# The rope's exchange of halves: a product with a signed permutation, or four transfers per head and kind

## The chip, the cores and the metric

The kernel runs on one core of a Trainium2 chip. The time is that of the device in microseconds (us); less is better. A core has TensorE (PE) for matrix products, VectorE (DVE), ScalarE (ACT) and GpSimd (POOL) for work on elements, and SyncE (SP), which here only sends transfers. ACT sends transfers too, from a queue of its own. Sums of products stand in PSUM, eight banks of 128 x 512 f32; everything else in SBUF, 128 partitions wide.

## The reference

Two layers of a transformer block with three branches over a latent sequence of 512 tokens and a context of 256: a gated convolution of 31 taps, a bidirectional chunked delta rule, and differential attention with 4 heads of two 64-wide parts. The change is in attention, in the rotary embedding (rope) of q and k, which only the 512 latent tokens get:

```python
def apply_rope(x, cos, sin):
    xf = x.astype(jnp.float32)
    half = xf.shape[-1] // 2
    rot = jnp.concatenate([-xf[..., half:], xf[..., :half]], axis=-1)
    return (xf * cos[:, None, None, :] + rot * sin[:, None, None, :]).astype(x.dtype)

    (conv_val, conv_glu, conv_z, dq, dk, dv, dz, dbeta, ddecay,
     aq, ak, av, az, mgate) = jnp.split(h @ w_in, IN_SPLITS, axis=-1)
    ...
    q_lat = apply_rope(qk_heads(aq, da_q_norm_g), cos, sin)
    k_lat = apply_rope(qk_heads(ak, da_k_norm_g), cos, sin)
    v_lat = av.reshape(B, S, DA_HEADS, 2 * DA_HEAD)
    o_da = diff_attention_latent(q_lat, k_lat, v_lat, k_ctx, v_ctx, lam)
    ...
    x_new = x + gate[:, None] * merge_branches(ys, mgate, w_branch, w_out)
```

`qk_heads` is an RMS norm over the 64 elements of each part. Within such a part rope needs the 32 elements of the one half beside those of the other, the sign of one of them turned.

## The kernel before

Channels lie on the partitions, tokens along the free axis. So one head's q is a tile of 128 partitions (two parts of 64) by 768 columns (512 latent tokens and 256 of context; in layer 1 the context has no q), and the exchange of halves moves rows of 32 partitions: 0-31 with 32-63, 64-95 with 96-127.

**Weights.** The projections are "units": one unit is 128 output channels, for which 512 KB of weights come by one transfer from SP into one of four buffers (`raw`, L845). ACT rounds them to a high part (`wHs`, L872), POOL or DVE takes the rest as a low part (`wLs`, L1973 on POOL in two halves, L1506 on DVE), and `dense` (L506) makes three products for each of eight blocks of input channels, 24 matmuls of 512 columns and, where the context belongs to it, as many of 256. A unit can start when both parts are there and the bank that it takes has been read. SP sends the weights of a unit when PE has ended the one four units before.

**Banks.** `product` (L417 to L435) gives every product the next one or two of the eight PSUM banks in turn and waits on PE until the bank's last product has been read by whoever reads it. The product of the exchange takes one bank in this round.

**One head.** For head h of layer l there are units for q, k and v; sums of squares per part (`allsum`, L521, with a block matrix) and their root on ACT (table loads L861, Ln L879, Exp L886); the norm on DVE (`an`, L1901) in place in `qh` or `kh`, which have two buffers each, by h % 2; and then the step `qrot`, the rope:
- PE: one product of the signed permutation `rot` with q or k (L798; the profile counts a 128x512 f32 product here as two instructions).
- DVE: `gm` = that product times the sine (L1911), reading the bank; it waits until the last use of `gm` is over.
- POOL: q or k times the cosine in place (L2095), then plus `gm` (L2098).

Cosine and sine are the table `cs`, loaded once per layer (L1210). Scores of a head (L552) wait for the rope of its q and k. Around them stand the softmax (maxima L1464 and L1467 on DVE, exponentials L906 on ACT, the mix L1488 and L1491 on DVE), the turn of the mixed weights (L529, copied by ACT at L1386 to `aT`), the product with the values (L565, copied by DVE at L484).

**Order.** `schedule` (L104 to L178) writes one list of steps for the whole program, and every engine walks the same list and issues its part of each step, so an engine's queue is in this order. While head h attends, the units and steps of head h + 1 are put in between: "q", "k", "sq", "v", "rq" (the exchange of q), "sk", "t", "rk" (the exchange of k). In these slots stand gate units too, whose logits are either made sigmoids of (L1240) or parked: ACT copies them (L1264) and sends them to DRAM (L1266), 256 or 384 KB. In layer 0 heads 2 and 3 get their exchanges beside parked units and pieces of the modulation vectors (`ada`, L999, L1444), in layer 1 "rq", "sk" and a parked unit are one slot, and "t", a parked unit and "rk" the next. ACT runs ahead of its steps where it prepares weights (`ahead`), as POOL does.

## Time and profile before

| | |
|---|---|
| runs (3), median | 1927.29 us |
| lowest, highest | 1923.66, 1928.23 us |
| profiled execution | 1927.93 us |
| its span | 1926.1 us |
| its mean granted TensorE clock | 0.973 of full speed |
| busy PE, DVE, ACT, POOL | 1799.3, 1127.7, 971.5, 669.2 us |
| bytes moved by transfers | 178.86 MB, 93 GB/s over the span |

Read it so. PE is busy nearly all the time, so both what PE does and what makes it wait set the end. The heads of attention are made in two stretches, about 485 to 835 us and 1495 to 1745 us from the span's start. Times of rows are starts from the start of the span; "[2.72 <-ACT Pa L906]" behind a row means that the engine stood idle so long before it, and what released it. A row without such brackets followed its forerunner on that engine at once.

### The profile page before, as it was taken

The page shows a single profiled execution, that of the slowest core. Times are in us where ns is not written, and L with a number is a line of the kernel's source. Part 1 is how long each engine was busy: PE and PEld are TensorE (multiplying, and loading weights), DVE is VectorE, ACT ScalarE, POOL GpSimd, SP SyncE. Part 2 cuts the span into 40 slices and gives each one's busy share as a digit, 9 for nine tenths or more (in the row PEclk, how much of TensorE's full clock was granted, in tenths as well). Part 3 has the DMA queues.
Part 4 walks back from the last instruction along what each step waited for, and adds up shares of the span by engine and source line. Part 5 has one row for each costly group of instructions (what it writes and reads, how often), then busy time and mean ns, then how long its engine had stood idle before and what let it go on. Part 6 is the DMA issues. An engine that isn't in the chain of part 4 may idle for free. (4 is left out here: it accounts for less than half of the span.)

```text
span 1926.1 us, 27717 instructions
## 1 busy us (share of the span) xinstructions
PE 1799.3 (93%) x11060; PEld 1497.2 (78%) x11060; DVE 1127.7 (59%) x1610; ACT 971.5 (50%) x1297; POOL 669.2 (35%) x490
## 2 busy tenths in 40 slices
PE   6789996899999999999999978999798999999999
PEld 5678886898888888888788857878696787777777
DVE  5556495459667656553234255749759866465343
ACT  6657523336445455553653156753337564555661
POOL 0011421537743434453153000144346544433150
PEclk9899998999999999999999999999799999999999
DMA  7123224422221122233244213324222221212352
GB/s 300 34 77 110 72 72 146 133 67 59 95 77 44 55 72 75 82 104 116 89 129 163 96 54 96 98 78 121 78 67 66 77 66 55 72 50 91 106 186 87
DMA packets 76414, 178.86 MB, mean 93 GB/s; under 512 B 6464, under 2 KB 29312, under 8 KB 76160
## 3 DMA queue, kind: packets, MB, share of 16 engines
q1 hardware_dynamic: 34272, 122.46, 20.6%
q10 hardware_dynamic: 42016, 54.63, 8.3%
q8 instruction: 89, 1.46, 0.3%
q14 instruction: 37, 0.30, 0.0%
HBM read 156.00 MB, written 21.07 MB: 92 GB/s over the span
## 5 line engine op out<-in xcount | busy, mean ns | idle before, releaser
L506 PE MATMUL banks<-hH,wHs 128*128 128x512 f32 x1984 | 599.0, 364 | 46.9 <-DVE hL L474 20.5
L506 PE MATMUL banks<-hH,wLs 128*128 128x512 f32 x1984 | 582.8, 355 | 0.0
L506 PE MATMUL banks<-hL,wHs 128*128 128x512 f32 x1984 | 581.1, 355 | 0.0
L1973 POOL TENSOR_TENSOR wLs<-raw,wHs 128x512 fp32r<-128x512 f32 x272 | 410.8, 1536 | 465.2 <-ACT wHs L872 465.2
L506 PEld LDWEIGHTS banks<-hH,wHs 128*128 128x128 f32 x1984 | 327.0, 191 | 123.6 <-issue 26.1
L506 PEld LDWEIGHTS banks<-hL,wHs 128*128 128x128 f32 x1984 | 324.8, 191 | 55.5 <-issue 2.2
L506 PEld LDWEIGHTS banks<-hH,wLs 128*128 128x128 f32 x1984 | 324.6, 191 | 54.7
L872 ACT ACTIVATE wHs<-raw 128x1024 fp32r<-128x1024 f32 x210 | 219.7, 1053 | 219.4 <-DMA raw<-wstream 219.2
L1529 DVE SCALAR_TENSOR_TENSOR acc<-padc,vecs,acc 128x783 f32<-128x783 f32 (+1 forms) x240 | 294.6, 1281 | 0.0
L861 ACT ACT_TABLE_LOAD x180 | 230.9, 1283 | 30.2 <-issue 13.0
L906 ACT ACTIVATE Pa<-banks,stat 128x768 f32<-128x768 f32 (+1 forms) x80 | 64.6, 813 | 144.0 <-DVE stat L1467 144.0
L1506 DVE TENSOR_TENSOR wLs<-raw,wHs 128x1024 fp32r<-128x1024 f32 x74 | 90.9, 1232 | 14.6 <-ACT wHs L872 14.5
L506 PE MATMUL banks<-yH,wHs 128*128 128x512 f32 (+1 forms) x288 | 89.8, 366 | 4.2 <-DVE gm L1850 1.8
L506 PE MATMUL banks<-yH,wLs 128*128 128x512 f32 (+1 forms) x288 | 88.0, 360 | 0.0
L506 PE MATMUL banks<-yL,wHs 128*128 128x512 f32 (+1 forms) x288 | 88.0, 360 | 0.0
L1464 DVE TENSOR_REDUCE stat<-banks 128x1 f32<-128x768 f32 (+1 forms) x80 | 64.0, 840 | 15.3 <-PE banks L552 15.1
L2079 POOL TENSOR_TENSOR mT<-mT,gm 128x768 f32<-128x768 f32 (+1 forms) x32 | 58.7, 1842 | 36.9 <-DVE gm L1850 36.9
L1193 ACT ACTIVATE vn<-banks,bcol 128x128 f32<-128x128 f32 x96 | 26.1, 381 | 77.8 <-DVE vs L1780 77.8
L1949 DVE SCALAR_TENSOR_TENSOR xs<-banks,ada,xs 128x512 f32<-128x512 f32 (+1 forms) x24 | 15.1, 658 | 83.2 <-PE banks L506 83.2
L552 PE MATMUL banks<-kh,qh 64*128 64x256 f32 (+1 forms) x288 | 55.6, 499 | 5.8 <-issue 5.6
L506 PEld LDWEIGHTS banks<-yH,wHs 128*128 128x128 f32 x288 | 47.9, 189 | 15.6 <-issue 3.9
L1491 DVE SCALAR_TENSOR_TENSOR Pa<-Pa,stat,Pa 128x768 f32<-128x768 f32 (+1 forms) x40 | 59.0, 1476 | 1.4
(242 smaller groups left out, 2330.8 us busy)
## 6 DMA issues: line engine op xcount, KB each, us to landing
raw<-wstream SPq DMA_DIRECT2D x210, 512.0 KB, 3.6
araw<-wstream SPq DMA_DIRECT2D x16, 512.0 KB, 12.6
E<-g_rows ACTq DMA_DIRECT2D x16, 384.0 KB, 7.0
egb<-eg_rows ACTq DMA_DIRECT2D x20, 256.0 KB, 4.2
inb<-intra_rows ACTq DMA_DIRECT2D x20, 256.0 KB, 4.5
parked_logits<-sg ACTq DMA_DIRECT2D x13, 384.0 KB, 4.1
xs<-xT SPq DMA_DIRECT2D x8, 384.0 KB, 11.4
intra_rows<-E ACTq DMA_DIRECT2D x8, 384.0 KB, 3.1
```

Of the source, the lines that this page charges most:

```text
L506: last = pe.matmul(out[:, a:b], w, m[:, kt, a:b], start=(kt == 0 and j == 0), stop=(kt == kts - 1 and j == 2))
L552: last = pe.matmul(outs[m][:, o:o + b - a], q_[r, qt * P:(qt + 1) * P], k_[r, a:b], start=True, stop=True)
L861: act.add_instruction(mybir.InstLoadActFuncSet(name=nc.get_next_instruction_name(), act_func_set_id=FUNCTION_SET[f], ins=[], outs=[]))
L872: act.activation(wH[w % RING][:, :], raw[w % RING][:, :], ACT.Copy).then_inc(*tick("act", "hi", v))
L906: act.activation(Pa[i][m][:, 0:w], place[key][:, 0:w], ACT.Exp, bias=stat[:, i, 2 + m:3 + m], accum_out=stat[:, i, 4 + m:5 + m]).then_inc( ...
L1193: ins = act.activation(vn[d][:, h, :], place[key][:, h * P:(h + 1) * P], ACT.Copy, scale=bcol[:, ORDER[d][s], 4 * d + h:4 * d + h + 1])
L1464: dve.tensor_reduce(stat[:, i, m:m + 1], place[key][:, 0:w], AX_X, ALU.max).then_inc(*tick("dve", "mx", l, h, qt, m))
L1491: dve.scalar_tensor_tensor(Pa[i][0][:, 0:w], Pa[i][0][:, 0:w], stat[:, i, 6:7], Pa[i][1][:, 0:w], ALU.mult, ALU.add).then_inc(*tick("dve", ...
L1506: dve.tensor_tensor(wL[w % RING][:, :], raw[w % RING][:, :], wH[w % RING][:, :].bitcast(F32), ALU.subtract).then_inc(*tick("dve", "lo", v))
L1529: ins = dve.scalar_tensor_tensor(acc[:, t, 0:W], padc[:, t, k:k + W], w, acc[:, t, 0:W], ALU.mult, ALU.add)
L1973: ins = pool.tensor_tensor(wL[w % RING][:, o:o + 512], raw[w % RING][:, o:o + 512], wH[w % RING][:, o:o + 512].bitcast(F32), ALU.subtract)
L2079: pool.tensor_tensor(mT[:, d, 0:n], mT[:, d, 0:n], gms[d % 2][:, 0:n], ALU.add).then_inc(*tick("pool", "gadd", l, n_, d))
```

## The change

The permutation and its product are gone. At the same step ACT now sends four transfers, each of 32 partitions by 512 tokens (64 KB), from `qh` or `kh` straight into `gm`, the half of one part into the place of the other: `o ^ 32` is the other half's first partition. Before them it waits for the norm of this tile (`an`), for the end of the rope before this one (the last reader of `gm`), and at the first exchange of layer 1 for an older use of the buffer. DVE waits for the fourth transfer and multiplies `gm` by the sine in place, POOL waits for that. The sign is in the sine table now, made on the host beside the other constants. PE has nothing to do at this step and takes no bank.

```diff
@@ -48,7 +48,7 @@
 NV = V_AL + 1

-C_ID, C_BLK, C_ROT, C_NEG = 0, 128, 256, 384
+C_ID, C_BLK, C_NEG = 0, 128, 256
 NCON = C_NEG + 2 * P
@@ -237,7 +237,7 @@
         stages = ["start"] + sorted({it[0] for it in ITEMS})
         names = ["%s_%s" % (e, k) for e in ("pe", "act", "dve", "pool") for k in stages]
-        names += ["w_high", "w_low_pool", "w_low_dve", "raw0", "raw1", "raw2", "raw3", "small_in", "c_in", "x_in", "x_out", "rope_in"]
+        names += ["w_high", "w_low_pool", "w_low_dve", "raw0", "raw1", "raw2", "raw3", "small_in", "c_in", "x_in", "x_out", "rope_in", "halves_in"]
         names += ["park_out0", "park_out1", "leaf_out0", "leaf_out1"] + ["park_in%d" % i for i in range(4)]
@@ -307,7 +307,6 @@
         ident = cons[:, C_ID:C_ID + P]
         blk = cons[:, C_BLK:C_BLK + P]
-        rot = cons[:, C_ROT:C_ROT + P]

@@ -791,12 +790,7 @@
                            lambda t: ("asq", kind, l, h), 1)
                 elif k == "qrot":
-                    h, kind = it[2], it[3]
-                    dst = (qh if kind == "aq" else kh)[h % 2]
-                    out = product(pe, ("rot", kind, l, h), SEQ)
-                    pe.wait_ge(*done("an", kind, l, h))
-                    pe.matmul(out[:, 0:SEQ], rot, dst[:, 0:SEQ], start=True,
-                              stop=True).then_inc(*tick("pe", "pe", ("rot", kind, l, h)))
+                    pass
                 elif k == "vunit":
@@ -850,6 +844,7 @@
             done_hi = [0]
             prev_ada = []
+            last_rope = []
             first_hi = [0]
@@ -1351,6 +1346,18 @@
                         act.wait_ge(*done("read", ("ak", l, h), 0))
                         act.activation(at1[0][:, 0:n], kh[h % 2][:, 0:n], ACT.Square).then_inc(*tick("act", "asq", "ak", l, h))
+                elif k == "qrot":
+                    h, kind = it[2], it[3]
+                    src = (qh if kind == "aq" else kh)[h % 2]
+                    act.wait_ge(*done("an", kind, l, h))
+                    if last_rope:
+                        act.wait_ge(*done("rope", *last_rope[-1]))
+                    if l and not (h or kind == "ak"):
+                        act.wait_ge(*done("gadd", l - 1, 0, KT - 2))
+                    last_rope.append((kind, l, h))
+                    for o in range(0, P, 32):
+                        act.dma_start(gm[o:o + 32, 0:SEQ], src[o ^ 32:(o ^ 32) + 32, 0:SEQ]).then_inc(
+                            *tick("halves_in", "half", kind, l, h, o, by=16))
                 elif k == "vunit":
@@ -1902,14 +1909,11 @@
                 elif k == "qrot":
                     h, kind = it[2], it[3]
-                    key = ("rot", kind, l, h)
-                    dve.wait_ge(*done("pe", key))
+                    dve.wait_ge(*done("half", kind, l, h, 96))
                     dve.wait_ge(*done("rope_in", l))
-                    if last_gm[0]:
-                        dve.wait_ge(*done(*last_gm[0]))
                     last_gm[0] = ("rope", kind, l, h)
-                    dve.tensor_tensor(gm[:, 0:SEQ], place[key][:, 0:SEQ], cs[:, 1, :],
-                                      ALU.mult).then_inc(*tick_read("dve", key))
+                    dve.tensor_tensor(gm[:, 0:SEQ], gm[:, 0:SEQ], cs[:, 1, :],
+                                      ALU.mult).then_inc(*tick("dve", "rots", kind, l, h))
                 elif k == "sc":
@@ -2091,7 +2095,7 @@
                     h, kind = it[2], it[3]
                     dst = (qh if kind == "aq" else kh)[h % 2]
-                    pool.wait_ge(*done("read", ("rot", kind, l, h), 0))
+                    pool.wait_ge(*done("rots", kind, l, h))
                     pool.tensor_tensor(dst[:, 0:SEQ], dst[:, 0:SEQ], cs[:, 0, :],
@@ -2169,12 +2173,6 @@
     con[:, C_ID:C_ID + P] = np.eye(P)
     con[:, C_BLK:C_BLK + P] = (i[:, None] // 64) == (i[None, :] // 64)
-    for m in range(P):
-        if m % 64 < 32:
-            con[m + 32, C_ROT + m] = -1.0
-        else:
-            con[m - 32, C_ROT + m] = 1.0
-
     con[:, C_NEG:C_NEG + P] = np.where(i[:, None] <= i[None, :], 0.0, -1e30)
@@ -2184,7 +2182,8 @@
     ang = np.concatenate([ang, ang], axis=-1).T
     ang = np.concatenate([ang, ang], axis=0)
-    rope = np.stack([np.cos(ang), np.sin(ang)], axis=1).astype(np.float32)
+    sign = np.where(i[:, None] % 64 < 32, -1.0, 1.0)
+    rope = np.stack([np.cos(ang), sign * np.sin(ang)], axis=1).astype(np.float32)
     return {"con": con, "rope": rope}
```

ScalarE's order in layer 1 where head 2's q is exchanged (`qh_164` is that q, `Pa` the softmax weights, `at` the root, `wHs` a unit's high part, `sg` parked logits), before:

```order
L906 ACTIVATE Pa_176,stat<-banks,stat 128x768 [waits pe_pv,dve_sc]
L906 ACTIVATE Pa_177,stat<-banks,stat 128x768 [waits pe_pv,dve_sc]
L861 ACT_TABLE_LOAD [waits dve_qsum]
L879 ACTIVATE at_1_172<-banks,misc 128x768 [waits pe_qsum]
L861 ACT_TABLE_LOAD
L886 ACTIVATE at_1_172<-at_1_172 128x768 [waits act_qsum]
L872 ACTIVATE wHs<-raw_52 128x1024 [waits pe_vunit,raw1]
L1264 ACTIVATE sg_137<-banks 128x512 [waits dve_branch,pe_park]
L1266 DMA parked_logits<-sg_137 128x512 [waits act_park]
```

and with the change:

```order
L901 ACTIVATE Pa_176,stat<-banks,stat 128x768 [waits pe_pv,dve_sc]
L901 ACTIVATE Pa_177,stat<-banks,stat 128x768 [waits pe_pv,dve_sc]
L1359 DMA gm<-qh_164 32x512 [waits pool_qrot,dve_qsum]
L1359 DMA gm<-qh_164 32x512 x3
L856 ACT_TABLE_LOAD [waits dve_qsum]
L874 ACTIVATE at_1_172<-banks,misc 128x768 [waits pe_qsum]
L856 ACT_TABLE_LOAD
L881 ACTIVATE at_1_172<-at_1_172 128x768 [waits act_qsum]
L867 ACTIVATE wHs<-raw_52 128x1024 [waits pe_vunit,raw1]
L1259 ACTIVATE sg_137<-banks 128x512 [waits dve_branch,pe_park]
L1261 DMA parked_logits<-sg_137 128x512 [waits act_park]
```

The four issues stand behind the exponentials and ahead of the table load for k's root; all that follows keeps its order.

TensorE's order at the same place (`L552` are the scores of head 1, `L521` the sum of squares of k, `L506` the unit behind them), before:

```order
L552 MATMUL banks<-kh_167,qh_165 128x512 [waits pool_qrot,act_vunit,act_qunit,act_qsum]
L552 MATMUL banks<-kh_167,qh_165 128x512
L552 MATMUL banks<-kh_167,qh_165 128x256 x2
L798 MATMUL banks<-qh_164,cons 128x512 [waits dve_qsum,act_pv]
L521 MATMUL banks<-at_0_171,cons 128x512 [waits act_qsum,act_sc,dve_pv]
L521 MATMUL banks<-at_0_171,cons 128x256
L506 MATMUL banks<-hH,wHs 128x512 [waits w_low_pool,w_high,act_sc]
```

and with the change, where these lines are L551, L520 and L505:

```order
L551 MATMUL banks<-kh_167,qh_165 128x512 [waits pool_qrot,act_vunit,act_qunit,act_qsum]
L551 MATMUL banks<-kh_167,qh_165 128x512
L551 MATMUL banks<-kh_167,qh_165 128x256 x2
L520 MATMUL banks<-at_0_171,cons 128x512 [waits act_qsum,act_pv]
L520 MATMUL banks<-at_0_171,cons 128x256
L505 MATMUL banks<-hH,wHs 128x512 [waits w_low_pool,w_high,dve_pv]
```

The product is gone, and with the round of banks moved by one the sum of squares and the unit wait for other readers: `dve_pv` is DVE's copy at L484, `act_sc` the exponentials, `act_pv` the copy of `aT`.

## Rows read from the trace of the kernel before

**Rows 1.** Page, section 1: busy us (share of the span) and instructions per engine.
```profile
PE 1799.3 (93%) x11060; PEld 1497.2 (78%) x11060; DVE 1127.7 (59%) x1610; ACT 971.5 (50%) x1297; POOL 669.2 (35%) x490
```

**Rows 2.** Busy us of each engine, summed over eight stretches with exchanges.
```profile
sum 600.00, PE 586.70 PEld 474.12 DVE 374.30 ACT 314.30 POOL 276.58; mean PE 73.34 PEld 59.27 DVE 46.79 ACT 39.29 POOL 34.57
```

**Rows 3.** Chain of waits, 1655 to 1670: start us, us, what.
```profile
1662.10 0.86 PE banks L798 x2
```

**Rows 4.** Timeline of PE, 1641 to 1650: start, us, instruction, idle before.
```profile
1648.22 0.50 PE L506 MATMUL banks<-hH,wHs 128*128 128x512 f32 x1 [2.72 <-ACT Pa L906]
```

**Rows 5.** Transfers: timeline of ACT's issues, query of L1266, page section 6.
```profile
1386.67 0.45 ACTq L955 DMA_DIRECT2D egb<-eg_rows  x1
1387.15 0.47 ACTq L957 DMA_DIRECT2D inb<-intra_rows  x1
...
L1266 ACTq DMA_DIRECT2D parked_logits<-sg x23: 326/326/352, 699.6 to 1786.4; - x23
...
DMA to landing us min/median/max: 2.0/4.1/5.7
...
parked_logits<-sg ACTq DMA_DIRECT2D x10, 256.0 KB, 3.9
```

**Rows 6.** Timelines of four engines, 532 to 545: layer 0, head 0.
```profile
532.87 0.37 ACT L999 ACTIVATE adar<-banks 4x256 f32<-4x256 f32 x1 [1.34 <-PE banks L582]
...
533.87 0.69 DVE L1911 TENSOR_TENSOR gm<-banks,cs 128x512 f32<-128x512 f32 x1 [0.70 <-PE banks L798]
...
538.61 6.50 POOL L1973 TENSOR_TENSOR wLs<-raw,wHs 128x512 fp32r<-128x512 f32 x4
...
543.71 0.61 PE L506 MATMUL banks<-hH,wHs 128*128 128x512 f32 x2
```

**Rows 7.** Timelines of ACT and PE, 609 to 621.5: layer 0, head 1's q.
```profile
618.13 0.81 ACT L1386 ACTIVATE aT<-banks 128x768 f32<-128x768 f32 x1
...
620.39 0.60 PE L506 MATMUL banks<-hH,wHs 128*128 128x512 f32 x2
```

**Rows 8.** Timelines of four engines, 693 to 706: layer 0, head 2's q.
```profile
695.55 1.05 ACT L872 ACTIVATE wHs<-raw 128x1024 fp32r<-128x1024 f32 x1
...
693.69 0.69 DVE L1911 TENSOR_TENSOR gm<-banks,cs 128x512 f32<-128x512 f32 x1
...
697.09 2.54 POOL L1973 TENSOR_TENSOR wLs<-raw,wHs 128x512 fp32r<-128x512 f32 x2
...
704.73 0.71 PE L506 MATMUL banks<-hH,wHs 128*128 128x512 f32 x2
```

**Rows 9.** Timelines of four engines, 1520 to 1529: layer 1, head 0's k.
```profile
1521.11 0.60 ACT L1240 ACTIVATE sg<-banks 128x512 f32<-128x512 f32 x1 [1.52 <-PE banks L506]
...
1521.96 0.69 DVE L1911 TENSOR_TENSOR gm<-banks,cs 128x512 f32<-128x512 f32 x1 [2.58 <-PE banks L798]
...
1524.54 1.64 POOL L2098 TENSOR_TENSOR kh<-kh,gm 128x512 f32<-128x512 f32 x1
...
1527.45 1.56 PE L552 MATMUL banks<-kh,qh 64*128 64x512 f32 x8
```

**Rows 10.** Timelines of ACT and PE, 1646.5 to 1658: layer 1, head 2's q.
```profile
1654.28 0.58 ACT L1264 ACTIVATE sg<-banks 128x512 f32<-128x512 f32 x1
...
1656.37 0.48 PE L506 MATMUL banks<-hH,wHs 128*128 128x512 f32 x1
```

**Rows 11.** Timelines of ACT and PE, 1722 to 1738: layer 1, head 3.
```profile
1723.03 1.04 ACT L872 ACTIVATE wHs<-raw 128x1024 fp32r<-128x1024 f32 x1
...
1734.11 0.33 ACTq L1266 DMA_DIRECT2D parked_logits<-sg  x1
...
1727.71 0.48 PE L506 MATMUL banks<-hH,wHs 128*128 128x512 f32 x1
...
1734.80 2.84 PE L565 MATMUL banks<-aT,Va 128*128 128x128 f32 x24
```

**Rows 12.** Stretch 1718.5 to 1721.9, after a wait: busy, PEclk, DMA share.
```profile
1718.50:1721.90 3.40, 3.40 (x10) 2.66 (x9) 0.00 (x0) 3.35 (x5) 1.61 (x2) 0.50 0.00 0
```

## The prediction

> **What bounds the kernel now.** I read the page first, for the share of each engine. The reader is to see that TensorE (PE) is busy 1799.3 us, 93% of the span, and that no other engine passes 59% [rows 1]. Then I cut out the eight stretches in which the heads of attention are prepared, with the table of busy time by stretch: 600 us in all, in which PE is busy 586.70 us, and VectorE (DVE), ScalarE (ACT) and GpSimd (POOL) 374.30, 314.30 and 276.58 us [rows 2]. So the first question is what goes from PE's row of work, and the second what makes PE wait after it. The timelines of the four engines at each exchange of halves answer the second. The profiled execution took 1927.93 us, 1.83 us more than its span; the sum is made against that, and the median of the runs (1927.29) is 0.64 us below it, less than the runs differ among themselves.
>
> **What goes.** Each exchange takes one product (two matmul instructions) from PE. The chain of waits gives its price where PE stands full before and after it: 0.86 us between two runs of 24 dense matmuls [rows 3]. There are 16 exchanges (two layers, four heads, q and k), so PE gets back 13.8 us at most. The product also took a PSUM bank in turn. Without it the following products meet other predecessors in the round of eight banks; in layer 1 the order shows that the unit behind head 2's exchange waits for an operation of `pv` in place of one of `sc`. Before, PE stands 2.72 us for that exponential [rows 4], and once more the same at head 3. That wait can go as well. What gets late next decides the sum.
>
> **What comes.** ACT issues four transfers of 64 KB, then DVE multiplies by the sine in place, then POOL does its two operations as before. Two sizes matter, and neither operation stands in the trace.
> I is ACT's time for four issues. Issues that follow one another start 0.48 us apart [rows 5], so I = 1.9 us; the single issue at L1266 takes 0.33 us [rows 5], so the lower bound is 4 x 0.33 = 1.3.
> L is the time from the first issue to the landing of the last quarter. Ends: three issues of 0.33 and the fastest landing of a parked block, 2.0 [rows 5], give 3.0; three pitches of 0.48 and its slowest, 5.7, give 7.1. The nearest row is the parked block of the same 256 KB from this queue, 3.9 [rows 5]; so L = 3.9, which leaves 2.5 us for the landing of the last quarter.
> The DVE multiply keeps its length, 0.69 us; its source is now SBUF. Weight loads are in flight at the same moments, since SP sends one whenever PE ends a unit; that is inside the bound of 7.1.
>
> At one place the Trainium skill is to be weighed. The row gives 3.9 for 256 KB in one transfer [rows 5]. "DMA: Bandwidth & Descriptors", section "Anatomy of one DMA — SWDGE (gpsimd) path", puts a transfer at some 2.0 us and its bytes at 436 GB/s, 2.15 us for 64 KB. If the four overlap, an estimate by it is L = 3 x 0.48 + 2.15 = 3.6, and the sum below would be 1.2 us smaller. "SBUF — State Buffer", section "The DMA setup-cost knee", speaks against the change: small transfers pay that fixed part each. Were the four to run one behind the other, L would be 8.6 and the sum 19 us larger. The issues 0.48 us apart show that a queue takes the next without waiting for the landing of the one before.
>
> **The places, one by one** (plus is later).
> Layer 0, head 0, both kinds in one stretch. The last ACT work before k's exchange waits for PE and ends at 533.24; PE comes 0.86 earlier without q's product, so ACT is free at 532.38. The sine multiply starts at 532.38 + 3.9 = 536.28 instead of 533.87, 2.41 later. POOL goes on gapless behind it: rope, then the low parts of weights, of which the unit at 543.71 needs the first two (half of the 6.50 in the row), done at 541.86 before and 544.27 now. Against 543.71: +0.56 [rows 6].
> Layer 0, head 1. At q ACT is gapless up to the copy of aT, done at 618.94; with I it is 620.84, and the unit's bank is that one's, started at 620.39 before: +0.45 [rows 7]. At k nothing is near: -0.86.
> Layer 0, head 2. At q ACT comes to the exchange at 695.55. The multiply moves from 693.69 to 699.45, 5.76 later. POOL's rope and two low parts end at 705.39 instead of 699.63, and PE wanted them at 704.73: +0.66 [rows 8]. What PE had gained before that is given back. k: -0.86. Head 3 of layer 0 has the same pattern, so again +0.66 - 0.86.
> Layer 1, head 0, both kinds. ACT is free at 1521.71 - 0.86 = 1520.85; the multiply starts at 1524.75 instead of 1521.96, 2.79 later; POOL's rope, done at 1526.18, is at 1528.97, and the scores stood at 1527.45: +1.52 [rows 9].
> Layer 1, head 1: both have cover, -1.72.
> Layer 1, head 2. At q ACT is gapless up to the copy of the parked logits, done at 1654.86; with I 1656.76, and the unit whose bank it frees started at 1656.37: +0.39. So the 2.72 us of [rows 4] are not gained, they turn into a wait for ACT [rows 10]. k: -0.86.
> Layer 1, head 3. At q ACT is done at 1724.07 + 1.9 = 1725.97, the copy of the logits with its 0.6 at 1726.57, and the unit that stood at 1727.71 can start 1.14 earlier. But k's issues now lie ahead of the last copy of aT: the parked transfer's issue ends at 1734.44 - 1.14 = 1733.30, I and the copy of 0.81 make it 1736.0, and the last twelve products with the values, half of the row at 1734.80, started at 1736.2. Net -0.1 [rows 11].
> Sum: 0.56 + 0.45 - 0.86 + 2 x (0.66 - 0.86) + 1.52 - 1.72 + 0.39 - 0.86 - 0.1 = -1.0 us: **1926.9 us**.
> The rest costs nothing by this count: the constants are 64 KB smaller at the start, where the load stands beside others; 16 x 256 KB = 4 MB more in transfers, spread over the stretches. Queued behind the waiting DVE multiply are convolution taps (two of them directly behind it at k of both heads 0) and statistics of the next scores; behind POOL's wait are low parts of weights. Queued behind ACT's wait for `an` is nothing that was not behind it before, since `an` is done by then.
> Four of the terms grow by L, three by I. At the lower ends: -1.0 - 4 x 0.9 - 3 x 0.6 = -6.4, 1921.5 us. At the upper: -1.0 + 4 x 3.2 = +11.8, 1939.7 us.
>
> **Rivals.**
> First, the gain stays: landing and issues lie at their lower ends, and PE keeps part of what the freed banks give. For it speaks that an issue alone is 0.33; against it that the issues in a row are 0.48 and that ACT is gapless at three of the places. Time: the sum at its lower end with one of the two waits of 2.72 kept is 1918.8; with nothing given back, 16 x 0.86 + 2 x 2.72 = 19.2, it would be 1908.7, which I do not expect. I take 1920.
> Second, slower: the exchange is on the path to the rope, and the last quarter lands late because weight loads of 512 KB are in flight. If it needs the 4.1 of a parked block [rows 5] behind three pitches, L is 5.5 and the sum +5.4; a new PE wait of that length can bring the clock down as it did once, when 3.4 us passed at 0.50 [rows 12], 1.7 us lost each time. Time: 1927.93 + 5.4 + 1.7 = 1935.0. It decides from L of about 5.6, where the sum alone passes the bound of 0.3%.
> Third, DVE: its multiply waits at the head of its queue, so the taps behind it come 2.4 to 2.8 us later. DVE is busy 374.30 of 600 us, which leaves room, yet the taps stand on the chain in places. Both heads 0 at full price: +5.2 - 1.0, 1932.1.
> That the change does not do what it says can't be much: the product is gone from PE's order at both places shown.
>
> **How the numbers follow.** Chances: forecast 0.40, first rival 0.22, second 0.26, third 0.12. A difference of 0.3% (5.8 us: below 1921.5, above 1933.1) is about what a measurement of this kernel can tell from no change. The forecast and the third rival fall within it, and about a sixth of the second; hence faster 0.22, same 0.54, slower 0.24. The range reaches from the first rival's 1919 to 1937, inside the upper end of L; the forecast's own range is 1922 to 1932.
>
> **What would show it.** In the changed profile: no PE row of the rotation; ACT issues of 0.33 to 0.48 us and their landings (L) in the table of transfers; the multiply by the sine idle before it for a DMA, 2 to 6 us at heads 0 and at q of heads 2 and 3 of layer 0; PE's waits for low parts of POOL in the unit behind the exchange of those q's, for the rope at the first scores of layer 1, and for ACT's copies at the two places of [rows 7] and [rows 10]. The prediction is wrong if the last quarter lands later than 5 us after the first issue, if PE's waits of 2.72 go without another in their place, or if the taps on DVE bring a later end of the convolution.

## The result and the profile after

The changed kernel took 1945.87 us (median of 4 runs, 1940.80 to 1948.45), the one before beside it 1927.30: ratio 1.0101, 95% interval 1.0086 to 1.0116. It is 19 us slower, where 1926.9 with a range to 1937 was forecast. The profiled execution has a span of 1943.4 us, 17.3 more than before.

The page after, section 1:

```profile
PE 1791.6 (92%) x11028; PEld 1495.9 (77%) x11028; DVE 1148.8 (59%) x1610; ACT 970.5 (50%) x1297; POOL 681.0 (35%) x490
```

Beside [rows 1] TensorE has 32 instructions and 7.7 us of busy time less: the sixteen products are gone. DVE is busy 21 us longer and POOL 12, with the same number of instructions. Next the rows of the four transfers' line: duration of an issue on ACT (ns, least, median, most), who waited, and the time from issue to landing.

```profile
L1359 ACTq DMA_DIRECT2D gm<-qh x32: 514/612/623, 502.6 to 1735.6; - x32
L1359 ACTq DMA_DIRECT2D gm<-kh x32: 514/612/1363, 531.0 to 1753.7; - x32
...
  DVE gm L1915: 68.0, 14
DMA to landing us min/median/max: 1.9/3.2/5.6
```

An issue takes 0.61 us, not the 0.45 of [rows 5], and DVE, which had waited 12.3 us for the product in all, waits 68.0 us for transfers at 14 of the 16 places. What that does to TensorE stands in the timelines of the four engines. Layer 0, head 0's k, to be laid beside [rows 6]:

```profile
530.97 3.19 ACTq L1359 DMA_DIRECT2D gm<-kh  x4
...
538.76 0.69 DVE L1915 TENSOR_TENSOR gm<-gm,cs 128x512 f32<-128x512 f32 x1 [7.58 <-DMA gm<-kh]
...
543.62 2.93 PE L551 MATMUL banks<-kh,qh 64*128 64x512 f32 x8 [4.16 <-POOL kh L2102]
547.53 0.58 PE L505 MATMUL banks<-hH,wHs 128*128 128x512 f32 x2 [0.98 <-POOL wLs L1977]
```

From the first issue to the multiply 7.8 us pass (L, the time from the first issue to the landing of the last quarter, was put at 3.9). TensorE stands 4.16 us at the scores, and the eight matmuls of the scores then take 2.93 us, where eight of the same shape took 1.56 in [rows 9]: the clock has fallen. Layer 0, head 2's q, beside [rows 8], with the fourth issue and SP's queue in the first lines:

```profile
698.89 0.61 ACTq L1359 DMA_DIRECT2D gm<-qh  x1
...
698.72 2.68 SPq L839 DMA_DIRECT2D raw<-wstream  x3
...
703.00 0.69 DVE L1915 TENSOR_TENSOR gm<-gm,cs 128x512 f32<-128x512 f32 x1 [6.43 <-DMA gm<-qh]
...
704.32 1.14 DVE L1495 TENSOR_SCALAR Pa<-Pa,c 128x768 f32<-128x768 f32 x1
705.49 1.90 DVE L1498 SCALAR_TENSOR_TENSOR Pa<-Pa,stat,Pa 128x768 f32<-128x768 f32 x1
...
707.52 3.78 DVE L1536 SCALAR_TENSOR_TENSOR acc<-padc,vecs,acc 128x783 f32<-128x783 f32 x2
...
706.54 3.92 POOL L1977 TENSOR_TENSOR wLs<-raw,wHs 128x512 fp32r<-128x512 f32 x2
...
710.61 0.98 PE L505 MATMUL banks<-hH,wHs 128*128 128x512 f32 x2 [5.02 <-POOL wLs L1977]
```

The first issue is at 697.05. SP's first weight load starts at 698.72, 0.2 us before the fourth quarter is issued; the first three quarters land 1.9 to 2.1 us after their issue, the fourth after 4.1, and the multiply waits for it. Then DVE's mix of the softmax runs beside POOL's rope, and two taps of the convolution beside POOL's low parts, which they did not before, and all get longer: the mix 1.90 us against 1.02, the two taps 3.78 against 1.97, the two low parts 3.92 against 2.54 [rows 8]. TensorE waits 5.02 us. Head 3 repeats this. Layer 1, head 2's q, beside [rows 4, 10], and head 3's k, beside [rows 11]:

```profile
1666.53 1.28 ACT L856 ACT_TABLE_LOAD   x1 [0.77 <-issue]
...
1671.73 0.58 ACT L1259 ACTIVATE sg<-banks 128x512 f32<-128x512 f32 x1
...
1672.36 0.50 PE L505 MATMUL banks<-hH,wHs 128*128 128x512 f32 x1 [2.71 <-ACT sg L1259]
...
1751.81 2.47 ACTq L1359 DMA_DIRECT2D gm<-kh  x4
1754.38 0.81 ACT L1393 ACTIVATE aT<-banks 128x768 f32<-128x768 f32 x1 [3.02 <-issue]
...
1755.29 0.98 PE L564 MATMUL banks<-aT,Va 128*128 128x128 f32 x3 [2.57 <-issue]
```

At q the issues run during ACT's exponentials, and 0.77 us of them is left. The wait for the exponential is gone, and one of the same size for ACT's copy of the parked logits stands in its place, as forecast. At head 3's k ACT's copy of aT waits for its queue to issue four transfers, and TensorE for that copy.

Last the clock: stretches in which the granted clock was 0.50 (length; busy us and instructions of PE, PEld, DVE, ACT, POOL; PEclk; DMA share; GB/s).

```profile
543.40:546.80 3.40, 2.93 (x8) 1.26 (x8) 3.40 (x3) 0.00 (x0) 3.40 (x3) 0.50 0.00 0
710.60:714.00 3.40, 3.39 (x11) 2.92 (x12) 1.53 (x4) 1.78 (x5) 0.00 (x0) 0.50 0.03 5
802.80:809.60 6.80, 4.41 (x14) 3.77 (x14) 3.91 (x5) 2.79 (x6) 2.25 (x2) 0.50 0.02 5
...
1741.40:1748.20 6.80, 6.13 (x14) 4.79 (x15) 6.69 (x8) 3.07 (x5) 6.15 (x4) 0.50 0.10 39
sum 34.00, PE 29.77 PEld 22.62 DVE 24.87 ACT 14.11 POOL 20.06; mean PE 3.72 PEld 2.83 DVE 3.11 ACT 1.76 POOL 2.51
```

There are eight such stretches among the heads, 34 us in which TensorE was busy 29.8 at 1.2 in place of 2.4 GHz. Before there was one, that of [rows 12]. TensorE has eight waits of 2.5 us or more in these stretches of the program, and each has a stretch at 0.50 at its end or within 1 us behind it.

Where the 17.3 us come in is seen from the start of the same TensorE instruction in both traces at the borders of each head. The clock's part is half of the busy time at 0.50 after, less the same of before; "other" is the rest.

| stretch | forecast | measured | clock | other |
|---|---|---|---|---|
| layer 0, head 0 | +0.6 | +4.9 | +1.5 | +3.5 |
| head 1 | -0.4 | -0.8 | 0 | -0.8 |
| head 2 | -0.2 | +4.4 | +1.7 | +2.7 |
| head 3 | -0.2 | +8.1 | +3.9 | +4.2 |
| layer 1, head 0 | +1.5 | +3.9 | +1.4 | +2.5 |
| head 1 | -1.7 | -1.2 | 0 | -1.2 |
| head 2 | -0.5 | 0.0 | +1.7 | -1.7 |
| head 3 | -0.1 | +4.1 | +3.0 | +1.1 |
| sum | -1.0 | +23.4 | +13.2 | +10.2 |

The rest of the program is 6 us shorter, mostly stretches at half clock that fell otherwise (one of 6.8 us near 1880 is missing after); run 1, without any exchange, shows 4 us of this too. Over the whole program the half clock costs 6.5 us more than before in this pair of traces, not 13.2.

### The profile page after: what moved, and what is told of

Same layout as the page of the kernel before. It is cut to its first block and busy times, and to the rows that moved or that the text cites. A ratio compares the mean times of both kernels' runs of the same rounds, so it can differ in the third digit from the quotient of the medians.

```text
span 1943.4 us, 27713 instructions
## 1 busy us (share of the span) xinstructions
PE 1791.6 (92%) x11028; PEld 1495.9 (77%) x11028; DVE 1148.8 (59%) x1610; ACT 970.5 (50%) x1297; POOL 681.0 (35%) x490
## 5 line engine op out<-in xcount | busy, mean ns | idle before, releaser
L505 PE MATMUL banks<-hH,wHs 128*128 128x512 f32 x1984 | 600.3, 364 | 54.7 <-DVE hL L473 18.8
L505 PE MATMUL banks<-hH,wLs 128*128 128x512 f32 x1984 | 582.5, 355 | 0.0
L505 PE MATMUL banks<-hL,wHs 128*128 128x512 f32 x1984 | 582.3, 355 | 0.0
L1977 POOL TENSOR_TENSOR wLs<-raw,wHs 128x512 fp32r<-128x512 f32 x272 | 420.7, 1572 | 426.6 <-ACT wHs L867 426.6
L505 PEld LDWEIGHTS banks<-hH,wHs 128*128 128x128 f32 x1984 | 327.6, 191 | 131.3 <-issue 40.5
L505 PEld LDWEIGHTS banks<-hL,wHs 128*128 128x128 f32 x1984 | 326.0, 192 | 55.0 <-issue 1.9
L505 PEld LDWEIGHTS banks<-hH,wLs 128*128 128x128 f32 x1984 | 325.6, 191 | 54.5
L1536 DVE SCALAR_TENSOR_TENSOR acc<-padc,vecs,acc 128x783 f32<-128x783 f32 (+1 forms) x240 | 311.0, 1348 | 0.0
L1513 DVE TENSOR_TENSOR wLs<-raw,wHs 128x1024 fp32r<-128x1024 f32 x74 | 90.9, 1233 | 14.2 <-ACT wHs L867 14.1
L505 PE MATMUL banks<-yH,wHs 128*128 128x512 f32 (+1 forms) x288 | 87.9, 359 | 4.2 <-DVE gm L1857 1.8
L505 PE MATMUL banks<-yH,wLs 128*128 128x512 f32 (+1 forms) x288 | 87.4, 358 | 0.0
L505 PE MATMUL banks<-yL,wHs 128*128 128x512 f32 (+1 forms) x288 | 87.4, 357 | 0.0
L1471 DVE TENSOR_REDUCE stat<-banks 128x1 f32<-128x768 f32 (+1 forms) x80 | 64.0, 840 | 17.3 <-PE banks L551 17.2
L551 PE MATMUL banks<-kh,qh 64*128 64x256 f32 (+1 forms) x288 | 58.3, 519 | 15.3 <-POOL kh L2102 8.3
```

The source lines that it names most:

```text
L505: last = pe.matmul(out[:, a:b], w, m[:, kt, a:b], start=(kt == 0 and j == 0), stop=(kt == kts - 1 and j == 2))
L551: last = pe.matmul(outs[m][:, o:o + b - a], q_[r, qt * P:(qt + 1) * P], k_[r, a:b], start=True, stop=True)
L1471: dve.tensor_reduce(stat[:, i, m:m + 1], place[key][:, 0:w], AX_X, ALU.max).then_inc(*tick("dve", "mx", l, h, qt, m))
L1513: dve.tensor_tensor(wL[w % RING][:, :], raw[w % RING][:, :], wH[w % RING][:, :].bitcast(F32), ALU.subtract).then_inc(*tick("dve", "lo", v))
L1536: ins = dve.scalar_tensor_tensor(acc[:, t, 0:W], padc[:, t, k:k + W], w, acc[:, t, 0:W], ALU.mult, ALU.add)
L1977: ins = pool.tensor_tensor(wL[w % RING][:, o:o + 512], raw[w % RING][:, o:o + 512], wH[w % RING][:, o:o + 512].bitcast(F32), ALU.subtract)
```

## Experiments

In the experiments two explanations stand against each other. Theory A: what costs is that the last quarter lands late where weight loads are in flight, that DVE, POOL and then TensorE queue behind it, and that the clock halves behind TensorE's waits. Theory B: the cost lies in ACT's issues and the moved round of banks. All ratios are to the kernel before, run beside each.

**Run 1, no exchange at all.** The exchange is left out: DVE multiplies q or k itself by the sine.

```diff
-                    for o in range(0, P, 32):
-                        act.dma_start(gm[o:o + 32, 0:SEQ], src[o ^ 32:(o ^ 32) + 32, 0:SEQ]).then_inc(
...
-                    dve.tensor_tensor(gm[:, 0:SEQ], gm[:, 0:SEQ], cs[:, 1, :],
+                    dve.tensor_tensor(gm[:, 0:SEQ], src[:, 0:SEQ], cs[:, 1, :],
```

> Leaves the exchange out: no product, no transfers, DVE multiplies q or k itself by the sine into gm as soon as the norm is there. What is left is the change without its price: the free bank and 0.86 us of TensorE at 16 places. Theory A (what costs are the transfers that land late, and the halved clock behind each wait): 16 x 0.86 = 13.8 us and part of the two waits of 2.72 come back, 1908 to 1916 us. Theory B (ACT's issues and the moved round of banks cost the time, the landing little): the banks' part stays, so over 1920 us.

Measured: 1904.59 us, ratio 0.9902 (0.9883 to 0.9921), a little under A's range. Head by head against before: -1.7, -1.9, -3.3, -3.3, -1.7, -1.9, -2.4, -2.0, in sum -18.1 us; 13.8 are the products, the other 4.3 are put down to the moved round of banks (run 7), which is thus a gain and not a cost, against B. No new stretch at half clock. The gain is there, and the transfers' price is 38 us between this run's ratio and the changed kernel's. The run does not part their issues from their landings, since both are gone. The wait for the copy of the parked logits in layer 1 is there without any issue:

```profile
1640.37 0.50 PE L505 MATMUL banks<-hH,wHs 128*128 128x512 f32 x1 [2.56 <-ACT sg L1259]
```

**Run 2, the same transfers issued early.** ACT issues each set as soon as the norm is done, at an earlier step of the list; DVE and POOL keep their steps. For q of layer 1's head 0 the norm is only just done, it stays.

```diff
+EARLY = {110: ("aq", 0, 0), 115: ("ak", 0, 0), 131: ("aq", 0, 1), 140: ("ak", 0, 1),
+         157: ("aq", 0, 2), 166: ("ak", 0, 2), 183: ("aq", 0, 3), 192: ("ak", 0, 3),
+         353: ("ak", 1, 0), 367: ("aq", 1, 1), 374: ("ak", 1, 1), 388: ("aq", 1, 2),
+         394: ("ak", 1, 2), 408: ("aq", 1, 3), 414: ("ak", 1, 3)}
...
+            def exchange(kind, l, h):
...
-            for it in ITEMS:
+            for ix, it in enumerate(ITEMS):
...
+                if ix in EARLY:
+                    exchange(*EARLY[ix])
```

> Same transfers, but ACT issues 15 of the 16 sets some 5 to 20 us sooner, when the norm is done (1 to 28 us ahead of the old place); all else stays at its step. Theory A: the landing is over when DVE comes to the multiply, so its waits for transfers (68 us in sum) nearly all go, the waits of TensorE at the scores and units behind go, and the clock falls with them: 1910 to 1920 us, faster than before. Theory B: the same 64 issues and the same banks remain, so 1940 us or more.

Measured: 1909.46 us, ratio 0.9925 (0.9907 to 0.9943), 14 us faster than before and, by the ratios, 34 faster than the changed kernel. The rows of its transfers, and the timelines of DVE, POOL and PE at head 2's q of layer 0:

```profile
L884 ACTq DMA_DIRECT2D gm<-qh x32: 514/612/633, 489.9 to 1697.9; - x32
...
  DVE gm L1925: 1.6, 1
DMA to landing us min/median/max: 1.9/2.7/4.9
...
688.27 0.69 DVE L1925 TENSOR_TENSOR gm<-gm,cs 128x512 f32<-128x512 f32 x1
...
691.67 2.51 POOL L1987 TENSOR_TENSOR wLs<-raw,wHs 128x512 fp32r<-128x512 f32 x2
...
696.49 0.71 PE L509 MATMUL banks<-hH,wHs 128*128 128x512 f32 x2
```

The landings are hardly shorter (median 2.7, most 4.9; 3.2 and 5.6 in the changed kernel), but only one is waited for, 1.6 us in place of 68.0. The two low parts take 2.51 us again and TensorE goes on without a wait. B is out as it stands: the 64 issues and the banks are the same. What an issue costs where ACT stands idle ahead of it (head 3's k above) is moved too, so the gain is that of the place of both, issues and landings.

**Run 3, product at six exchanges, transfers at ten.**

```diff
+PRODUCT = {("aq", 0, 0), ("ak", 0, 0), ("aq", 0, 2), ("aq", 0, 3), ("aq", 1, 0), ("ak", 1, 0)}
...
+                    if (kind, l, h) in PRODUCT:
...
```

> Product for six exchanges (both kinds of head 0 in both layers, q of heads 2 and 3 of layer 0), transfers for the other ten. Theory A: the places where the trace after shows the loss (+4.9, +4.4, +8.1, +3.9 us) mostly go, what stays is head 3 of layer 1 (+4.1) and the gains of 0.86 at covered ones: 1923 to 1931 us. Theory B: ten sixteenths of the loss stay, 1936 to 1941 us.

Measured: 1926.62 us, ratio 1.0014 (0.9998 to 1.0029). The six carry the loss: with them back, heads 0 are at 0.0, and heads 2 and 3 of layer 0 at +0.8 and +0.6.

**Run 4, one transfer per exchange.**

```diff
-                    for o in range(0, P, 32):
-                        act.dma_start(gm[o:o + 32, 0:SEQ], src[o ^ 32:(o ^ 32) + 32, 0:SEQ]).then_inc(
-                            *tick("halves_in", "half", kind, l, h, o, by=16))
+                    act.dma_start(gm[:, 0:SEQ], src[:, 0:SEQ]).then_inc(
+                        *tick("halves_in", "half", kind, l, h, 96, by=16))
```

> One transfer of 256 KB in place of four of 64 KB, as a plain copy of q or k into gm (the halves are not exchanged); same bytes, same waits. ACT issues 0.6 us in place of 2.5 and the last byte is issued 1.9 us sooner. Theory A: L falls by 1.5 to 2 us to 2.5 (nothing else in flight) to 5.5 us; at the four places on the rope's path TensorE gets 1.5 to 2 us each and some of the clock: 1928 to 1938 us. If a weight load in flight is what delays the landing, L stays over 4 us where one is. Theory B: the issues' part goes, 1925 to 1930 us.

Measured: 1919.14 us, ratio 0.9978 (0.9965 to 0.9991), below both ranges and nearer to B's. The edit shortens issues and landing at once, so the time alone does not part the theories; the landings speak for A.

```profile
L1358 ACTq DMA_DIRECT2D gm<-qh x8: 472/472/535, 501.9 to 1713.4; - x8
L1358 ACTq DMA_DIRECT2D gm<-kh x8: 472/475/1339, 530.1 to 1729.5; - x8
...
  DVE gm L1914: 41.7, 13
DMA to landing us min/median/max: 2.2/3.2/6.0
```

The same 256 KB land in 2.2 to 2.3 us at all eight q's, where no weight load starts more than 0.6 us before the landing, and in 4.1 to 6.0 at the k's, with 504 to 1304 KB of weights in flight. At heads 2 and 3 of layer 0 the edit turns +4.4 and +8.1 into -1.4 and -1.5: there the transfer at q is now over before the loads that had caught the fourth quarter. The loads in flight and the three further issues are both in L.

**Runs 5 and 11, products whose result is thrown away, in TensorE's waits.** Run 5, and under it run 11, which differs in the table alone. It also fills the unit behind head 0's scores, where run 5 kept a wait of 2.35 us and a stretch at 0.50:

```diff
+FILL = {("gate2", 0, 3): 5, ("gate2", 0, 6): 5, ("gate0", 0, 1): 3}
...
+            def idle(pe, out, n):
+                for _ in range(n):
+                    pe.matmul(out[:, 0:SEQ], blk, cons[:, 0:SEQ], start=True, stop=True)
...
+                if h == 0 and qt == 0:
+                    idle(pe, outs[0], 4)
...
+                if u in FILL:
+                    idle(pe, out, FILL[u])
```

```diff
-FILL = {("gate2", 0, 3): 5, ("gate2", 0, 6): 5, ("gate0", 0, 1): 3}
+FILL = {("aq", 0, 1): 1, ("gate2", 0, 4): 5, ("gate2", 0, 7): 5, ("gate0", 0, 2): 3}
```

> The changed kernel with products whose result is thrown away (128x512 f32, 0.86 us each) ahead of five waits of TensorE: four before the first scores of head 0 in each layer, five, five and three before the units behind the waits of 5.02, 5.02 and 3.08 us in layer 0. They lie inside those waits. Theory A with its second half (part of the loss is the clock at half speed behind a wait): no window of 0.50 behind these five, about 8.5 us back, 1935 to 1940 us. If the clock is not a part of the loss, the same 1946 us or, where a product outlasts its wait, a little more.

Measured: 1934.91 us, ratio 1.0062 (1.0042 to 1.0082), against 1.0101 for the changed kernel. The time fits, the reason does not: I had named the wrong units. The products at heads 2 and 3 ran at 692 to 697 us, far ahead of the wait, and delayed the end of the unit that releases SP's loads from 698.7 to 705.3. So the fourth quarter landed alone (L 3.8 and 4.0 in place of 5.9 and 6.1). The waits of 5.02 us are gone in this run, but by earlier landings and ten added products at once, so it does not tell what the clock is worth.

> Run e5 put ten of its products one unit too soon at heads 2 and 3 of layer 0: they did not lie in the waits of 5.02 us but 15 us ahead, and made SP send its loads later, behind the quarters. Here the same kernel with the products at the right places: four before the first scores of head 0 in each layer, one before the unit behind, five each before the two units that waited 5.02 us, three before the one that waited 3.08. Landings as in the changed kernel (5.9 and 6.1 us at q of heads 2 and 3). If the clock is part of the loss by itself: no half clock at these places, 1.5 + 1.7 + 3.9 + 1.4 = 8.5 us back, 1935 to 1940 us. If run e5 gained by the moved loads alone: 1944 to 1948 us.

Measured: 1934.63 us, ratio 1.0061 (1.0042 to 1.0081), with the landings of the changed kernel (5.99 and 6.14 us at those two q's). PE's timeline at head 2's q, and the stretches behind the four former waits of layer 0 and layer 1's head 0:

```profile
701.64 4.03 PE L512 MATMUL banks<-cons 128*128 128x512 f32 x9
706.41 0.58 PE L506 MATMUL banks<-hH,wHs 128*128 128x512 f32 x2 [0.74 <-POOL wLs L1986]
...
540.00:548.00 8.00, 6.71 (x37) 4.99 (x34) 7.97 (x7) 2.67 (x5) 8.00 (x6) 1.00 0.00 0
704.00:714.00 10.00, 9.26 (x48) 7.04 (x46) 4.50 (x6) 5.94 (x9) 2.26 (x2) 1.00 0.01 2
790.00:812.00 22.00, 20.82 (x115) 15.47 (x113) 14.56 (x20) 10.77 (x16) 11.30 (x8) 1.00 0.37 119
852.00:864.00 12.00, 12.00 (x71) 9.85 (x71) 9.92 (x11) 6.34 (x9) 7.76 (x5) 1.00 0.36 121
1535.00:1550.00 15.00, 15.00 (x78) 11.91 (x78) 13.69 (x21) 6.76 (x12) 6.97 (x5) 1.00 0.12 36
```

The clock is 1.00 in all five. The late weights still hold the units up (0.74 us of the wait is left), and the "other" part is hardly changed: +4.4, +2.9, +3.8 and, at layer 1's head 0, +2.6, where the changed kernel had +3.5, +2.7, +4.2, +2.5. The 7.7 us between the ratios go with the clock, 8.5 by the table above. Head 3 of layer 1, where nothing was filled in, still has its half clock. But a wait does not always bring one: in this run the wait at layer 1, head 2's q, is as long as in the changed kernel, and the clock stays at 1.00 behind it, while a stretch at 0.50 stands at 1621.9 to 1625.3 behind a wait of 1.95 us:

```profile
1660.77 0.50 PE L506 MATMUL banks<-hH,wHs 128*128 128x512 f32 x1 [2.71 <-ACT sg L1268]
```

**Run 6, weight loads held until the quarters have landed.**

```diff
+HOLD = {56: ("ak", 0, 0), 66: ("ak", 0, 1), 72: ("aq", 0, 2), 76: ("ak", 0, 2), 83: ("aq", 0, 3), 87: ("ak", 0, 3),
+        161: ("aq", 1, 0), 163: ("ak", 1, 0), 170: ("aq", 1, 1), 172: ("ak", 1, 1), 178: ("aq", 1, 2), 179: ("ak", 1, 2),
+        185: ("aq", 1, 3), 186: ("ak", 1, 3)}
...
+                if w in HOLD:
+                    sp.wait_ge(*done("half", *HOLD[w], 96))
```

> The changed kernel with 14 weight loads held back on SP until the four transfers of an exchange near them have landed (those issued within 2.5 us before to 3.5 us after the exchange). Theory A, that weights in flight make the landing late: every set lands 3.9 us after its first issue as the undisturbed ones do, in place of 4.7 to 7.8; TensorE's waits for rope and low parts shrink by 2 to 4 us at four places, 1930 to 1937 us unless held weights come too late for a unit. If the landing is late for another reason, L stays at 5 to 8 us and so does the time.

Measured: 1941.92 us, ratio 1.0102 (1.0078 to 1.0126).

```profile
  DVE gm L1920: 49.6, 13
DMA to landing us min/median/max: 1.9/2.0/3.7
...
1679.95 1.41 PE L567 MATMUL banks<-aT,Va 128*128 128x128 f32 x5 [4.14 <-issue]
```

The cause of the late landing is shown: the median of a quarter is 2.0 us, and 13 of 16 sets land 3.8 to 4.0 us after their first issue. The time does not follow. Layer 0 gets its part ("other" +2.8 us over its four heads in place of +9.6), but layer 1 loses: held weights come late on ACT (8.04 us idle for them), TensorE waits 4.14 us at 1679.95, and head 2 stands at +6.6 in place of 0.0. The half clock costs 8.6 us in layer 1's heads, 7.8 in the changed kernel. A transfer that is spared a collision moves it elsewhere. And not all of the wait at the q's of heads 2 and 3 in layer 0 is L's: with L at 3.8 and 4.0 TensorE still waits 3.49 and 3.40 us there for the low parts, which take 3.92 us as in the changed kernel.

**Run 7, run 2 with the old round of banks.**

```diff
                 elif k == "qrot":
-                    pass
+                    bank_next[0] = (bank_next[0] + 1) % 8
```

> Run e2 (early issue) with the old round of banks: at each exchange one bank is passed over, as if the product still took it. Shows what the moved round is worth. From e2's gains of 3.3 us at heads 2 and 3 of layer 0 and 2.1 to 2.4 us at those of layer 1, against 1.72 us of products: 1.5 + 1.5 + 0.6 + 0.4 = 4 us lost, 1913 to 1914 us. If banks do not matter, 1909.5.

Measured: 1915.69 us, ratio 0.9962 (0.9949 to 0.9976). Of run 2's 14 us gain the moved round of banks is about half: in the trace 6 us over the heads, most of it at heads 2 and 3 of layer 0 (-1.0 and +0.3 in place of -3.3 each; 1.7 of head 3's is a stretch at 0.50). In the kernel before, TensorE waits there for a bank that DVE has still to copy:

```profile
689.98 0.62 PE L506 MATMUL banks<-hH,wHs 128*128 128x512 f32 x2 [1.71 <-DVE at L484]
```

In run 7 the same wait is 2.76 us; in run 1 it is gone.

**Run 8, run 2 with eight transfers of 16 partitions.**

```diff
-                for o in range(0, P, 32):
-                    act.dma_start(gm[o:o + 32, 0:SEQ], src[o ^ 32:(o ^ 32) + 32, 0:SEQ]).then_inc(
+                for o in range(0, P, 16):
+                    act.dma_start(gm[o:o + 16, 0:SEQ], src[o ^ 32:(o ^ 32) + 16, 0:SEQ]).then_inc(
...
-                    dve.wait_ge(*done("half", kind, l, h, 96))
+                    dve.wait_ge(*done("half", kind, l, h, 112))
```

> Run e2 with eight transfers of 16 partitions (32 KB) in place of four of 32: ACT issues for 5.1 us in place of 2.5 at each exchange, and the last lands 2.6 us later. Theory A: with the early place both are covered, 1909 to 1913 us. Theory B (issues on ACT cost by themselves): 16 x 2.6 us more on ACT, at least a third of it on the path, over 1920 us.

Measured: 1913.95 us, ratio 0.9954 (0.9938 to 0.9970). Six heads stand within 0.3 us of where run 2 had them; the 5.6 us more lie at both heads 0, where the early place has less to spare (+0.2 in place of -1.7, +4.5 in place of -0.5). Twice the issues cost nothing where there is cover.

**Run 9, low parts ahead of POOL's wait.**

```diff
+                    if (kind, l, h) in (("aq", 0, 2), ("aq", 0, 3)):
+                        ahead(("gate2", 0, 3 * h - 3))
                     pool.wait_ge(*done("rots", kind, l, h))
```

> The changed kernel, but at q of heads 2 and 3 of layer 0 POOL makes the low parts of the next unit ahead of its wait for the sine, not behind it. L stays at about 6 us there. Theory A (the loss comes through what is queued behind the late landing): the two waits of 5.02 us go, and with them about 2 x 1.7 us of halved clock; the low parts take 2.5 us for two again in place of 3.9, since they no longer coincide with DVE's mix. 5.0 + 5.0 + 3.4 = 13 us back, less where the next scores or head 3's units take over: 1930 to 1936 us. If the landing delays TensorE by another way than POOL's queue, 1946 us as before.

Measured: 1940.32 us, ratio 1.0064 (1.0051 to 1.0077); 7 us back, about half of what was expected. Head 2's q of layer 0, on POOL, DVE, ACT and PE:

```profile
702.35 2.49 POOL L1977 TENSOR_TENSOR wLs<-raw,wHs 128x512 fp32r<-128x512 f32 x2 [9.66 <-ACT wHs L867]
...
704.79 0.69 DVE L1915 TENSOR_TENSOR gm<-gm,cs 128x512 f32<-128x512 f32 x1 [6.60 <-DMA gm<-qh]
...
707.28 1.92 DVE L1498 SCALAR_TENSOR_TENSOR Pa<-Pa,stat,Pa 128x768 f32<-128x768 f32 x1
...
712.19 0.48 ACT L901 ACTIVATE Pa<-banks,stat 128x256 f32<-128x256 f32 x1 [7.70 <-DVE stat L1474]
...
721.18 0.87 PE L528 MATMUL banks<-cons,vr 128*128 128x128 f32 x6 [2.69 <-ACT sg L1259]
```

Heads 2 and 3 stand at +3.6 and +2.4 in place of +4.4 and +8.1. The two waits of 5.02 us are gone and the low parts take 2.49 us, so they had been long only beside DVE's work. But the landing also stands at the head of DVE's queue: the mix and the maxima behind it are late, so are the exponentials on ACT (7.70 us idle), and TensorE waits 2.7 us for ACT later. So there were two ways from the landing to TensorE, one through POOL's queue and one through DVE's.

**Run 10, eight transfers at the late place.** The edit of run 8 on the changed kernel.

> The changed kernel with eight transfers of 16 partitions in place of four of 32, at the old, late place: L and ACT's issue both grow by 2.6 us. Run e8 showed the same eight at the early place at 4 to 5 us over run e2. Theory A: the four places on the path get 2.6 us each, ACT's three up to 2.6 each, with more of the clock: 1960 to 1972 us. If size of L did not matter, 1950 us.

Measured: 1976.87 us, ratio 1.0262 (1.0246 to 1.0277), more than expected.

```profile
710.90 0.69 DVE L1915 TENSOR_TENSOR gm<-gm,cs 128x512 f32<-128x512 f32 x1 [11.08 <-DMA gm<-qh]
```

Four more issues per set cost 31 us here and 5.6 at the early place. At q of heads 2 and 3 in layer 0 L did not grow by 2.6 us but by 4.9 and 4.6 (first issue at 700.02, multiply at 710.90), since five of the eight landed late beside the weight loads there (3.4 to 6.5 us), where it had been one of four. These heads stand at +14.2 and +12.0, of which 7.0 and 4.9 are the clock.

## Why the prediction was wrong

The step that failed is the size of L at the places where it counts. "The nearest row is the parked block of the same 256 KB" gave 3.9 us. Where no weight load was issued ahead of the last quarter that came out to a tenth: four sets landed 3.9 us after their first issue. This is luck in part, two errors that cancel: three pitches took 1.9 us and not 1.44, the last quarter 2.0 and not 2.5. But it was taken for all places, and collision with weight loads was left to the upper bound and a rival. At the places on the rope's path L was 7.8 (layer 0, head 0's k), 5.9 and 6.1 (q of heads 2 and 3) and 5.3 (layer 1, head 0's k). The prediction's own sign of being wrong, a last quarter later than 5 us, came at ten of the sixteen sets. SP's next load is released when TensorE ends a unit, and the exchanges lie near such ends: at layer 1, head 0's k, the load starts with the first issue (1534.3), at head 2's q of layer 0 just before the fourth.

By the forecast's own sensitivity the four places add 3.9 + 2.0 + 2.2 + 1.4 = 9.5 us to its -1.0: +8.5, against +10.2 measured without the clock. Place by place it fits less well: +4.5, +1.8, +2.0 and +2.9 by this count, +3.5, +2.7, +4.2 and +2.5 measured. Even the upper bound of 7.1 was too low at two k's, 7.8 and 7.5. The slowest landing, 5.6, stayed within the 5.7 assumed; but three pitches had been put at 1.44 and came to 2.6 at the first of the two, where one issue took 1.36 us. Run 6 shows the cause, runs 2 and 10 the effect.

The second failure is the clock. The row at 0.50 was in [rows 12] and had been priced at 1.7 us for one place in one rival. It came at seven new stretches and made 13.2 of the 23.4 us. In the changed kernel each of TensorE's waits over 2.5 us brought one, also those of 2.7 us. That is not certain for a wait of this length: the one in [rows 4] before, that of 2.71 in run 11 and that of 2.56 in run 1 brought none. Run 11 shows this part for itself.

The third is the durations taken over unchanged: two low parts at 2.54 us, measured 3.92 beside DVE's taps; runs 2 and 9 have 2.5 where they do not coincide, and run 6 has 3.92 with L at 3.8, so this failed apart from L.

What held: the products' 0.86 us (run 1); the waits named for low parts at q of heads 2 and 3, for the rope at the first scores of layer 1, and for ACT's copies (2.71 us in layer 1, 1.07 at head 1's q of layer 0). In layer 0, head 0, the path was another one than priced: the sum took the unit behind the scores, TensorE stood at the scores themselves (4.16 us) and 0.98 us more at the unit. The 2.72 us did turn into a wait for ACT, but hardly through I (ACT's time for four issues): run 1, without issues, waits 2.56 us at the same unit. The sum looked for the freed banks only there; run 7 puts their larger part at heads 2 and 3 of layer 0. I, forecast as 1.9 us of ACT, is 2.5 where ACT stands idle ahead of it (layer 1, head 3's k, 3.02 us to the next copy). Where ACT is behind with its exponentials, its queue issues during them, and 0.8 us was left at q of heads 2 and 3 in layer 1.

Of the rivals the second was the right one, with its mechanism. At 1935.0 it was too small, since it took 5.5 for L and one fall of the clock. The third named DVE's queue, with convolution taps at both heads 0; run 9 shows that queue at work at heads 2 and 3, with the softmax in it. The first did not happen; its bound of 19.2 us is close to the 18.1 of run 1 by luck, since it counted 5.4 us for the two waits of 2.72, which stay, and nothing for layer 0's banks.

The Trainium skill's page "SBUF — State Buffer", section "The DMA setup-cost knee", says that every transfer pays a fixed 2 us or so. The prediction's estimate from it, for four running one behind the other, was L = 8.6 and a sum 19 us larger, just the time measured. That is a coincidence: where no weights were in flight each quarter landed 2.0 us after its own issue, beside the others, and the set after 3.9. The estimate of 2.15 us for one of 64 KB, by the Trainium skill's page "DMA: Bandwidth & Descriptors", section "Anatomy of one DMA — SWDGE (gpsimd) path", agrees with that.

What stays open is why runs of one kernel differ by up to 1%. The traces show that stretches at half clock fall differently outside the heads; whether that is all of it was not tried.

## What to carry over

A transfer in place of a product is cheap only if its issue is parted from its use: the same 64 transfers cost 19 us where they are issued at the step that needs them and gain 14 (ratio 0.9925) where fifteen of the sixteen sets are issued when their source is ready. Price a transfer by what the same event sets off on other queues, not by its row alone. A new wait of TensorE in a stretch that was full is to be counted with the half clock that can follow it: here 13.2 us over the heads, on top of the 28.3 us by which they are longer without the clock than in run 1 (+10.2 against -18.1).

## What the runs showed of the hardware

- A 64 KB transfer within SBUF of 32 partitions landed 1.9 to 2.1 us after its issue when alone, 2.8 to 5.6 with one to three weight loads of 512 KB under way (changed kernel); one of 256 KB over 128 partitions 2.3 us alone (run 4), 4.1 to 6.0 beside weights.
- Issues in a row from ACT's queue were 0.64 us apart, against 0.48 for other transfers before. They ran while ACT's engine was busy with exponentials (0.77 us of 2.5 left at layer 1, head 2's q).
- POOL's pair of 128x512 subtractions took 2.5 us alone and 3.9 beside two DVE operations of 128x783, which took 3.78 against 1.97; DVE's mix of 128x768 took 1.90 beside POOL's rope against 1.02.
- Twenty-two products whose result is thrown away, 19 us of matmuls put into or beside waits, made the changed kernel 7.7 us shorter (run 11).
